# Two sliding attentions and a layer norm: evacuations, sums and filler products in another order

## The reference, cut to what matters

```
q = apply_rope(rms_norm(q.reshape(B, S, SW_KV_HEADS, SW_GROUP, HEAD_DIM), q_norm), cos, sin)
s = einsum('bnqhgd,bnkhd->bnhgqk', qb, kw) / sqrt(HEAD_DIM);  s = where(valid, s, NEG_INF)
m = maximum(max(s, axis=-1), sink);  e = exp(s - m);  p = e / (sum(e) + exp(sink - m))
o = einsum('bnhgqk,bnkhd->bnqhgd', p, vw);  return o.reshape(B, S, SW_HEADS * HEAD_DIM) @ w_o
```

```
y_a = g_b * dwconv(g_c * u_a, conv_a)
u = dwconv(v_b * sigmoid(gate_b), conv_b) + conv_b_bias
mu = mean(u);  var = mean(square(u - mu));  y_b = silu((u - mu) * rsqrt(var + EPS) * g + b)
return concatenate([y_a, y_b], axis=-1) @ w_out
```

## Time and profile before

| what | us |
|---|---|
| median of three runs | 2844.53 |
| the profiled execution | 2835.67 |
| its span | 2833.8 |
| TensorE busy, products | 2718.5 (96%) |
| TensorE busy, weight loads | 2247.3 (79%) |
| VectorE busy | 1734.1 (61%) |
| ScalarE busy | 1105.4 (39%) |
| GpSimd busy | 153.6 (5%) |

### The profile page before, as it was taken

How to read it: one execution, slowest core, us unless ns; L and a number is a source line. 1 busy time by engine, 2 the same in 40 slices (tenths; PEclk the granted TensorE clock), 3 DMA queues, 4 the chain that set the end, 5 groups by cost and what they waited for, 6 DMA issues and landing times.

```text
span 2833.8 us, 41990 instructions
## 1 busy us (share of the span) xinstructions
PE 2718.5 (96%) x14771; PEld 2247.3 (79%) x14771; DVE 1734.1 (61%) x2709; ACT 1105.4 (39%) x1869; POOL 153.6 (5%) x201
## 2 busy tenths in 40 slices
PE   7998999999888999999998999999999998999998
PEld 6897788888656788887887888888888776788886
DVE  7775677676654676768884654453455554664545
ACT  6554322224763323233423332232233665442432
POOL 5221000000110000000210000000000000000000
PEclk9999999999999999999998999999999999999999
DMA  4121354442012354532741112112111000222221
GB/s 140 60 75 60 137 181 172 170 161 86 16 46 90 137 189 159 182 134 68 168 117 45 45 61 74 60 60 68 56 51 58 16 31 31 82 97 97 97 86 63
DMA packets 75220, 263.76 MB, mean 93 GB/s; under 512 B 8496, under 2 KB 10800, under 8 KB 73264
## 3 DMA queue, kind: packets, MB, share of 16 engines
q1 hardware_dynamic: 70880, 249.99, 25.5%
q0 software_dynamic: 4176, 11.63, 2.2%
HBM read 247.87 MB, written 2.10 MB: 88 GB/s over the span
## 4 chain that ended last, share of the span: by engine, by line
PE 64%; issue 15%; DVE 10%; ACT 7%; DVEq 2%; ACTq 1%; POOLq 1%; POOL 0%
PE psum L1932 17%; PE psum L1934 17%; PE psum L1933 17%; DVE w_lo L1303 2%; ACT work L1104 2%; DVE work L1473 2%; ACT sw_pt L1116 1%; ACT w_hi L761 1%; PE psum L2075 1%; PE psum L2076 1%; PE psum L2077 1%; PE psum L2365 1%; PE psum L2268 1%; PE psum L2325 1%; DVE work L1591 1%
## 5 line engine op out<-in xcount | busy, mean ns | idle before, releaser
L1932 PE MATMUL psum<-hx_hi,w_hi 128*128 128x512 f32 x1568 | 623.1, 397 | 4.9 <-DVE hc_lo L1582 1.7
L1934 PE MATMUL psum<-hx_hi,w_lo 128*128 128x512 f32 x1568 | 620.6, 396 | 0.0
L1933 PE MATMUL psum<-hx_lo,w_hi 128*128 128x512 f32 x1568 | 620.1, 395 | 0.0
L761 ACT ACTIVATE w_hi<-w_raw 128x1024 fp32r<-128x1024 f32 (+1 forms) x328 | 344.7, 1051 | 508.9 <-PE psum L1934 217.1
L1303 DVE TENSOR_TENSOR w_lo<-w_raw,w_hi 128x1024 fp32r<-128x1024 f32 (+1 forms) x328 | 398.1, 1214 | 201.6 <-ACT w_hi L761 183.8
L1934 PEld LDWEIGHTS psum<-hx_hi,w_lo 128*128 128x128 f32 x1568 | 295.0, 188 | 70.2
L1932 PEld LDWEIGHTS psum<-hx_hi,w_hi 128*128 128x128 f32 x1568 | 295.0, 188 | 63.8 <-issue 5.2
L1933 PEld LDWEIGHTS psum<-hx_lo,w_hi 128*128 128x128 f32 x1568 | 295.1, 188 | 47.5
L1932 PE MATMUL psum<-a_hi,w_hi 128*128 128x512 f32 (+1 forms) x656 | 233.2, 355 | 9.3 <-DVE a_lo L1413 9.0
L1933 PE MATMUL psum<-a_lo,w_hi 128*128 128x512 f32 (+1 forms) x656 | 232.6, 355 | 0.0
L1934 PE MATMUL psum<-a_hi,w_lo 128*128 128x512 f32 (+1 forms) x656 | 232.4, 354 | 0.0
(11 more groups left out here) (294 smaller groups left out, 4605.2 us busy)
## 6 DMA issues: line engine op xcount, KB each, us to landing
mod_w<-in_w_mod SPq DMA_DIRECT2D x96, 512.0 KB, 3.6
w_raw<-in_fup SPq DMA_DIRECT2D x88, 512.0 KB, 4.4
w_raw<-in_cup SPq DMA_DIRECT2D x88, 512.0 KB, 3.2
w_raw<-in_fdown SPq DMA_DIRECT2D x32, 512.0 KB, 4.6
w_raw<-in_cdown SPq DMA_DIRECT2D x32, 512.0 KB, 3.2
sw_vb<-tap_prod POOLq DMA_DIRECT2D x29, 391.5 KB, 5.1
w_raw<-in_da_qkv SPq DMA_DIRECT2D x18, 512.0 KB, 3.8
w_raw<-in_fdown SPq DMA_DIRECT2D x16, 384.0 KB, 3.3
```

What stands on the lines that cost most here:

```text
L761: r = act.activation(w_hi[:, off:off + n], w_raw[:, raw:raw + n], ACT.Copy)
L1932: pe.matmul(dst, wh, xh, start=first, stop=False)
L1933: pe.matmul(dst, wh, xl, start=False, stop=False)
L1934: return pe.matmul(dst, wl, xh, start=False, stop=last)
```

## The change

**Sliding attentions.** On ScalarE evac_proj(m + 3) now stands in the odd slot, between `turned(m + 2)` and `outs(m - 1)`, instead of evac_proj(m + 2) at the head of the even slot. "pje" is released by the copy alone; then comes a drain, and the square reads the copy in SBUF and releases a new semaphore "sqr", for which VectorE waits before it sums the squares. On TensorE the mask is always added after the scores, the four tiles of a projection are issued in one piece, ahead of the turned queries, and all values follow behind the transposes.

**Layer norm.** The channel sums of tiles 0 to 2 are made ahead of the last quarter of `pair`. The squares have four buffers. The sums of squares move 128 columns of ones in place of one. Three groups of constant products are added.

```diff
 ScalarE
-                    if j >= 2:
-                        act.wait_ge(s_ln["ss"], j - 1)
-                    act.activation(wk[:, j % 2, 0:ALL], conv_out[:, j, :], ACT.Square).then_inc(s_ln["sq"], 1)
+                    act.activation(wk[:, j, 0:ALL], conv_out[:, j, :], ACT.Square).then_inc(s_ln["sq"], 1)
...
-                    r = act.activation(sw_raw[:, m % 2, :], pb[:, 0, 0:256], ACT.Copy, scale=root)
+                    act.activation(sw_raw[:, m % 2, :], pb[:, 0, 0:256], ACT.Copy, scale=root).then_inc(S["pje"], 1)
+                    act.drain()
                     if not st["ctx"]:
-                        r = act.activation(squares_of(m)[:, :, :, 0:HD], pb[:, 0, 0:256].rearrange("p (a b f) -> p a b f", a=2, b=2),
-                                           ACT.Square, scale=root)
-                    r.then_inc(S["pje"], 1)
-                    act.drain()
+                        act.activation(squares_of(m)[:, :, :, 0:HD], sw_raw[:, m % 2, :].rearrange("p (a b f) -> p a b f", a=2, b=2),
+                                       ACT.Square).then_inc(S["sqr"], 1)
+                        act.drain()
...
-                    if half == 0 and m < 14:
-                        evac_proj(m + 2)
+                    if p == 0:
+                        evac_proj(2)
...
                     if half and m < 14:
                         turned(m + 2)
+                    if half and m < 13:
+                        evac_proj(m + 3)
                     if half and m:
                         outs(m - 1)
 VectorE
-                dve.wait_ge(s_ln["ss"], 4)
-                dve.tensor_scalar(tok_ms[:, 0:6], ps_lin(3, ALL, ALL + 6), 1.0 / 512, EPS, ALU.mult, ALU.add)\
+                dve.wait_ge(s_ln["ss"], 1)
+                dve.tensor_scalar(tok_ms[:, 0:6], ps_lin(3).rearrange("p (t n) -> p t n", t=6)[:, :, 0], 1.0 / 512, EPS, ALU.mult, ALU.add)\
...
+                        dve.wait_ge(S["sqr"], m + 1)
 TensorE, layer norm
-                pair(st["after"], 0, 4)
+                def channel_sums(tiles):
+                    for a, b, c in segs(ALL):
+                        for j in tiles:
+                            r = pe.matmul(ps_lin(2, a, b), ones[:], conv_out[:, j, a:b], start=j == 0, stop=j == 3)
+                    return r
+
+                pair(st["after"], 0, 3)
+                pe.wait_ge(s_ln["conv"], 3)
+                pe.wait_ge(s_ev, st["lin0"] + 3)
+                channel_sums(range(3))
+                pair(st["after"], 3, 4)
                 pe.wait_ge(s_ln["conv"], 4)
+                channel_sums((3,)).then_inc(s_ln["mu"], 1)
                 pe.wait_ge(s_ev, st["lin0"] + 4)
...
+                keep_busy(6, 10)
                 for j in range(4):
                     pe.wait_ge(s_ln["sq"], j + 1)
                     for t in range(6):
-                        r = pe.matmul(ps_lin(3, ALL + t, ALL + t + 1), wk[:, j % 2, t * P:(t + 1) * P], ones[:, 0:1],
-                                      start=j == 0 and t == 0, stop=j == 3, skip_group_check=True)
-                    r.then_inc(s_ln["ss"], 1)
+                        r = pe.matmul(ps_lin(3, t * P, (t + 1) * P), wk[:, j, t * P:(t + 1) * P], ones[:],
+                                      start=j == 0 and t in (0, 4), stop=j == 3, skip_group_check=True)
+                r.then_inc(s_ln["ss"], 1)
+                keep_busy(4, 10)
                 pe.wait_ge(s_ln["pw"], 1)
                 spread(ALL, s_ln["rb"])
+                keep_busy(4, 18)
 TensorE, sliding attentions
-                    return pe.matmul(dst, ident_b[:], mask, start=start, stop=not start)
+                    return pe.matmul(dst, ident_b[:], mask, start=False, stop=True)
...
-                        r = pe.matmul(psum[:, w0:w0 + n], q[x], k[x][:, k0:k0 + n], start=bool(st["ctx"]), stop=not st["ctx"])
+                        r = pe.matmul(psum[:, w0:w0 + n], q[x], k[x][:, k0:k0 + n], start=True, stop=False)
...
-                    if half and m < 14:
-                        turn_q(m + 2)
                     if m < 13:
-                        project(m + 3, k0, k0 + (4 if st["ctx"] else 2))
+                        project(m + 3, k0, k0 + 4)
...
+                    if half and m < 14:
+                        turn_q(m + 2)
+                    if parts > 2:
+                        turn(p - 1, 2)
+                    for c in range(parts):
                         values(p - 1, c)
```

More of the change, by code:

```diff
@@ L332, in program @@
                     "kpe", "khi", "pje", "rot", "qhi", "ex", "ete", "invb", "ohi", "sinke",
-                    "krms", "krope", "rms", "rope", "mx", "sinkx", "inv", "invw", "osb", "olo", "kpr", "pr", "whi")
-        only_a = ("krms", "kpr", "rms", "pr")
+                    "krms", "krope", "sqr", "rms", "rope", "mx", "sinkx", "inv", "invw", "osb", "olo", "kpr", "pr", "whi")
+        only_a = ("krms", "kpr", "sqr", "rms", "pr")
         s_swt = {t: {k: sem(f"sw{t}_{k}") for k in sw_names if t == "a" or k not in only_a}
@@ L2293, in turn_q, with masked @@
                     r.then_inc(S["trq"], 1)
-                def masked(st, t, w0, start):
+                def masked(st, t, w0):
                     if not st["ctx"]:
@@ L2317, in scores @@
                         pe.wait_ge(S["ex"], p - 1)
-                    if not st["ctx"]:
-                        for x in range(2):
-                            masked(st, t, span(st, p, x)[0], True)
                     q = [sw_q[HD * x:HD * x + HD, m % 2, P * (p % 2):P * (p % 2) + P] for x in range(2)]
@@ L2331, in scores @@
                             pe.matmul(psum[:, w1 - CTX:w1], q[x], k[x][:, SEQ:ALL], start=True, stop=True)
[L2332 to L2335, removed]
+                    for x in range(2):
+                        r = masked(st, t, span(st, p, x)[0])
+                        if st["ctx"] or x == 1:
+                            r.then_inc(S["sc"], 1)
                 def turn(p, c):
```

## The result

The changed kernel has a median of 2825.94 us against 2841.92 us for the kernel before, five runs each: ratio 0.9939, 95% interval 0.9922 to 0.9955. The forecast was 2832.0, with a range of 2819 to 2843. Two executions of that comparison, 2996.48 us of the kernel before and 6732.42 us of the version at_out_late, lie far above the others and are left out. The profiled executions differ by 13.4 us (2835.67 and 2822.30), where the prediction's sum was 12.5.

What follows compares the result with a forecast made beforehand. TensorE, busy 96% of the span, was taken as the bound, so only its stalls or slow stretches could give time. Norm -12.0, first attention +2.0, second -2.5 sum to -12.5 us: from median 2844.53 to 2832.0, range 2819 to 2843.

Steps and rivals of the forecast that it cites:

- Steps 1 to 6: Layer norm, from early channel sums through wide sums to the next stage's first product: 10.5 us less.
- step 7: Stage after the layer norm: its first 3.0 us at half clock return 1.5 us.
- step 5: Layer norm: 48 wide records at 0.11 us each take 5.3 us plus a 0.3 tail.
- The order of o_hi: First attention: o_hi behind evacuation and square delays exponentials by 1.10 us; taken as +0.4 over 12 periods, +4.8 us.
- the 2.9: First attention: 2.9 us saved as the spread-out's long waits in two periods with a fallen TensorE clock go.
- No wait of TensorE for the evacuation: First attention, sign of being right: TensorE's wait for the emptied bank, 13.8 us in 12 waits, is gone.
- exponentials that wait for neg_max behind o_lo: First attention, sign of being right: ScalarE's exponentials wait for neg_max some 0.8 us a period, neg_max behind o_lo.
- The step named: Second attention: turned queries no longer wait for the weights' copy, 4.8 us in 14 waits; half taken, -2.5 us.
- (1): Layer norm: the clock still falls, 2835.5 us, or 2847 at half clock all the way; chance 0.20 for both.
- (2): Both attentions: the waits return in full, 13.8 and 4.8 us, giving 2814; chance 0.10.
- (3): Both attentions: o_hi's delay passes on in full, +14.3 and +6.0 us, 2852.8; decides from 0.95 a period; chance 0.07.
- (4): Layer norm: weight loads are not hidden in the wide sums, 5.3 us less gain, 2837.3; chance 0.05.

Runs made afterwards that it cites:

- at_out_late: at_low_max with, in the first attention, o_hi behind the exponentials and o_lo behind the next odd slot's maxima; ratio to the kernel before 0.9917.
- at_outs_oldrel: at_outs_first with the bank released only behind the square, which reads PSUM as before; first attention to the 15th normalised output 141.11 us.
- at_low_late: Changed kernel with VectorE's o_lo behind the maxima and rotation; first attention to the 15th normalised output 135.81 us, against 144.74.
- after_again: The changed kernel itself, timed again in the second comparison; median 2832.24 us, ratio 0.9954 to the kernel before.
- b_turn_old: Changed kernel with TensorE's turned queries ahead of the projection again in the second attention alone; first maxima to first addition into X 204.09 us, against 202.11.
- at_outs_first: Changed kernel with ScalarE's o_hi copy ahead of the evacuation in both attentions; first attention to the 15th normalised output 137.19 us, against 144.74.
- at_low_max: at_low_late with, in the first attention, the normalised output also behind the maxima; first attention to the 15th normalised output 133.57 us.
- ln_late: Changed kernel with all 16 channel-sum records behind the fourth tile's products again; layer norm stretch 42.38 us, against 37.97.

## Why the prediction was right, point by point

**Layer norm: -12 predicted, -10.1 measured.** Steps 1 to 6 came as worked out, 0.5 to 0.7 us late: channel sums done 1491.84 (1491.3), wide sums from 1493.76 (1493.2) and 5.64 long (5.6), next product 1505.94 (1505.2), clock 1.00 throughout. Half a microsecond was lost before it began: VectorE's next pass over the last convolution tile starts 0.63 us behind the row before it, 0.15 before, and the row names no releaser but issue:

```profile
1478.13 1.03 DVE L1473 SCALAR_TENSOR_TENSOR work<-work,vec 128x783 f32<-128x783 f32 x1 [0.63 <-issue]
```

In at_outs_oldrel, whose VectorE program has one wait less, LN is 0.57 shorter and the first centring 0.48 earlier; what the pause is stays open.

The step that failed is step 7, the 1.5 us that full clock was to return in the next stage. LN up to the first product is 9.69 us shorter (39.09 and 29.40), up to the first addition 10.13: it returned 0.44. TensorE itself did return most of it: the seven groups of products ahead of that addition run from 1515.72 to 1524.69 before (8.97 us) and from 1505.94 to 1513.78 after (7.84), 1.13 less. But the prediction did not ask what is late next. Before, the addition waits for TensorE; after, VectorE writes w_lo until 1514.42, and the addition follows with no wait (before, then after):

```profile
1524.73 1.14 DVE L1377 SCALAR_TENSOR_TENSOR X<-psum,mods,X 128x512 f32<-128x512 f32 x2 [0.62 <-PE psum L1934]
```

```profile
1513.19 1.23 DVE L1303 TENSOR_TENSOR w_lo<-w_raw,w_hi 128x1024 fp32r<-128x1024 f32 x1
...
1514.51 1.14 DVE L1377 SCALAR_TENSOR_TENSOR X<-psum,mods,X 128x512 f32<-128x512 f32 x2
```

Ahead of it stand the low parts of the four tiles, a chain of ScalarE and VectorE that full clock doesn't shorten: from the first to the fourth it takes 6.17 us before and 6.24 after.

The 48 wide records took 0.117 each with 5.43 us of weight loads beside them. By the rule cited at step 5, from the Trainium skill, page "TensorE: Matmul & The Clock Gate", section "The mechanism", by which a load overlaps products only where the row groups differ, they would, by the estimate made there, have taken twice as long; the measurement decides against it for these records of full height. The same section also lets a load run ahead when it targets the background weight buffer; the trace doesn't show which way the loads took, only that they did not add to the time.

**First attention: +2 predicted, +0.4 in AX and +2.5 in A15 measured** (up to +3.3 in AX in other executions). The period came out almost to the hundredth: o_hi at +1.57 (1.56), exponentials at +3.56 (3.56), outputs 2.16 behind them (2.1), second exponentials 1.54 later (1.54), the period 0.65 longer (0.6). But two terms of the sum were each too small. The order of o_hi costs 7.5 us and not 4.8; the rest of the change gives 5.1 and not 2.9. Their errors, 2.7 and 2.2, nearly cancel: that the sum came close is luck. And the 2.9 was put down to two clock falls that would go. It is the spread-out's wait that went, 10.2 to 0.9 us, in nearly all periods. Of the two falls one went (0.60 in 781.20 to 785.50 before) and one stayed (0.57 in 829 to 833, before and after), and later ones came, as in the last of these windows of the trace after:

```profile
781.00:785.00 4.00, 2.98 (x27) 2.09 (x26) 3.38 (x10) 3.50 (x10) 1.12 (x1) 1.00 0.01 2
829.00:833.00 4.00, 4.00 (x26) 2.99 (x25) 2.81 (x8) 2.46 (x7) 1.12 (x1) 0.57 0.01 4
841.00:845.00 4.00, 4.00 (x18) 2.54 (x19) 3.38 (x9) 1.97 (x6) 1.11 (x1) 0.50 0.00 0
```

"No wait of TensorE for the evacuation" was wrong as a sign: 10.4 us in 12 waits remain, while the loop through o_lo and the maxima ends later (at_low_late). The prediction's other sign, exponentials that wait for neg_max behind o_lo, was the right one.

That AX shows only +0.4 has another reason, the stretch from the 15th normalised output to the first addition into X, here before, after and in after_again:

```profile
862.60:883.36 20.76, 18.76 (x83) 14.78 (x84) 3.73 (x11) 3.33 (x9) 0.65 (x1) 0.84 0.07 26
```

```profile
864.16:882.83 18.67, 16.45 (x84) 12.94 (x84) 3.73 (x11) 3.37 (x10) 0.65 (x1) 1.00 0.10 30
```

```profile
864.90:886.10 21.20, 18.89 (x83) 14.92 (x84) 3.73 (x12) 3.33 (x9) 0.65 (x1) 0.84 0.08 26
```

In the profiled execution of the changed kernel it ran at full clock and took 18.67 us; in the other five it took 19.90 to 21.20, at a clock of 0.84 to 0.91. By those the first attention became 1.4 to 3.3 us longer in AX.

**Second attention: -2.5 predicted, -2.1 measured.** The step named is the one that gives it (b_turn_old). Part of the 4.8 us came back as TensorE's waits for the weights' copies ahead of the values, which went from 7.4 to 10.9 us; not all waits need lie on the path, and they do not add up to the 2.1. o_hi behind the evacuation costs nothing here (at_outs_first: BX 202.24).

**The sum.** In the profiled pair, -10.1 + 0.4 - 2.1 = -11.8 of 13.3 us of span; the other 1.5 lie where nothing was changed. The +0.4 rests on the full clock behind the 15th output; with the AX of the other executions (+1.4 to +3.3) the three sum to -10.8 to -8.9. The median of the first comparison fell by 16.0 us, of the second by 11.8; the predicted 12.5 lies between them, and whole runs can't say more. The forecast time, 2832.0, was added to the median of three runs, which two more runs lowered by 2.6.

**The rivals.** None came. The clock held in the norm (1). The waits did not return in full (2): even at_low_max, with o_lo and the output behind the maxima, has A15 8.7, AX 12.5 and BX 2.1 us below the kernel before, where the rival has 13.8 and 4.8. The delay of o_hi did not pass on in full (3): its order costs 7.5 us and not 14.3, and the other edits pay 5.1 back. The rival's threshold does not come out of its own prices: at 0.95 us a period they give about +6.4 us, and at the full 1.10 they give +8.3, both less than the 8.5 that the prediction calls the least that can be told from no change. The weight loads were hidden (4).

## What to carry to other kernels

When an instruction is moved ahead on an in-order engine, follow what it displaces: the copy behind it may release a small job on another engine that stands ahead of the one everybody waits for. Such a job, with no reader near, belongs behind the urgent one; here that was worth 8.9 us, more than the released bank gave (3.9), and it could not be seen before the move (1.0 us). And when a stall or a half clock goes, ask in the next stage too what is late next.

## What the runs showed of the hardware

A stretch of the convolution FFN of the second model, which no kernel here changes, runs at two speeds: from the norm's first addition into X to the second attention's first maxima it takes 680.2 to 681.0 us in four profiled executions (before, after, ln_late, at_low_max) and 687.0 to 688.1 in the others, of the same kernels too. In 100 us of it TensorE is 100% busy and its granted clock is 1.00 in both. The mean product of one group there takes 339 ns in place of 336, in after and then in at_low_late (last columns: busy us, mean ns of one, idle before):

```profile
L1935 PE MATMUL psum<-a_hi,w_lo 128*128 128x512 f32 (+1 forms) x128 | 43.1, 336 | 0.0
```

```profile
L1935 PE MATMUL psum<-a_hi,w_lo 128*128 128x512 f32 (+1 forms) x128 | 43.4, 339 | 0.0
```

The 7 us are about half of the spread of the whole runs. The profiled pair lies at the fast speed on both sides. The cause is open.
